# An encoder layer in float32: the chunked scans with one product for outputs and next state, and group norm by row sums

## The chip, the cores and the metric

One core of a Trainium2 chip runs the whole layer in one launch. The time is the device time of that core in microseconds. All matrix products are float32: a plain float32 product is issued as two instruction pairs (weight load and product), and the large ones are split by hand into a high and a low part.

## The reference, cut to what matters

```python
def rwkv7_branch(...):                       # T = 256 tokens, 16 heads of 64 channels
    ...
    o = wkv7_bidirectional(both(r_h), heads(decay), k_dir, both(v_h), both(kk), heads(a))
    mean = jnp.mean(o, axis=-1, keepdims=True)
    var = jnp.mean(jnp.square(o - mean), axis=-1, keepdims=True)
    o = ((o - mean) * lax.rsqrt(var + RWKV_GN_EPS)).reshape(B, T, RWKV_WIDTH)
    o = (o * gn_w.astype(jnp.float32) + gn_b.astype(jnp.float32)).astype(r.dtype)
    ...
    return (o + bonus) * g
```

`wkv7_bidirectional` is a linear recurrence over tokens with a 64x64 state per head, run forward and backward; the two results are added, the backward one turned round in time. What the layer does before it (a SwiGLU block, the input projection) and after it (the branch products with `w_branch_a` and `w_branch_b`, `w_out`, another SwiGLU block) is not touched.

## The kernel before, in words

Each engine has its own program; they meet at semaphores. Nearly all of the span is products of 128x128 weights with 512 moving columns (lines 1496 to 1498), whose matrices the SP queue loads into a ring of four slots; ScalarE makes the high part (`split_hi`, line 496) and VectorE the low part (`split_lo`, line 938). The next loads wait for the low part.

The scans are a stage of their own, 1328 to 1464 us. There are NM = 16 scans: m//2 is the pair of heads, m%2 the direction. A scan is cut into four chunks of 64 tokens. Data lie as channels by tokens (two heads on 128 partitions); for a backward scan the operands are stored or read in reversed order. For scan m:

- A (`alpha_beta`, lines 1785 and 1786) makes four 64x64 matrices per chunk and head; VectorE multiplies them by masks into `mb` (`masked_ab`, line 1352). Their decay ends come from `ends` (line 1251), which must be done before A of that scan (`dd_ready`).
- W (`w_products`, line 1811) multiplies them by the inverses `zs`; ScalarE copies the result with a minus sign into `wt` (`minus_w`, line 841).
- V (`values_t`, line 1801) turns the values by a product with the identity, chunk by chunk; ScalarE copies them beneath the state in `sv` (`values`, line 836).
- G (`gh_products`, lines 1826 and 1827) makes, per chunk and head, the matrix that takes state and values to outputs (64 columns) and to the next state (64 columns); VectorE masks it into `gh` (`masked_gh`, line 1361, two instructions of 128x512).
- R (`recur`) runs chunk after chunk: line 1842 multiplies `gh` by `sv` for the next state, which ScalarE copies into `sv` (line 869), and line 1846 multiplies `sv` by `gh` for the outputs, channels by tokens. VectorE brings outputs to `oc` (`to_oc`, lines 1370 and 1372), the backward ones reversed and added.

Group norm follows per pair of heads. `gn_means` and `gn_variances` (lines 1855, 1859) multiply `oc` and its squares by `headsum`, a matrix that adds the channels of a head and spreads the sum; VectorE subtracts (line 1318), ScalarE takes the square root over 128x256 (line 854), VectorE its reciprocal (line 1325), scales, adds and gates (lines 1326 to 1330). Then ScalarE and VectorE split the result into `yahi` and `yalo` (lines 859, 1334), weights of the branch product `p_ya`.

All is one order written out by hand. TensorE, for each m: W(m+1), V(m+1), then four times R(m,c) and A(m+2,c), with a group-norm product behind R(m,0), then G(m+1). VectorE, for each m: `ends(m+2)`, the two halves of `masked_ab(m+2)` with a part of the group norm between them (`norm_between`), `to_oc(m)`, the two halves of `masked_gh(m+1)`, and for m < 4 a weight split of `p_ya` (`ahead`). ScalarE, for each m: `minus_w(m+1)`, `values(m+1)`, three state copies, for m < 4 a weight split, and a part of the group norm. POOL loads values, bonus and gate per pair and copies `ik` and `vrev`.

Of the kernel before, what the change touches and what calls it, by code (L numbers as in the profile page):

```python
# [42 lines left out]
P = 128  # L43
# [45 lines left out]
def constants():  # L89
# [11 lines left out]
    k[:, K_MG:K_RESET] = np.concatenate([(p < C) | (s <= t), s >= -1 + 0 * t], 1)  # L101
# [10 lines left out]
def layer(nc, a, out):  # L112
# [94 lines left out]
    with ctx:  # L207
# [19 lines left out]
        def room(*names):  # L227
# [7 lines left out]
        s_g, (_, bo, gg, _, osq, rs) = room(("u_gap0", [P, NPAIR, T]), ("bo", [P, 4, T]), ("gg", [P, 4, T]),  # L235
                                            ("u_gap1", [P, NPAIR, T]), ("osq", [P, 2, T]), ("rs", [P, 2, T]))
# [4 lines left out]
        def ffn_room(tag):  # L241
# [93 lines left out]
        gn_mean, gn_cent, gn_sq, gn_var, gn_sqrt, ya_y, ya_hi, ya_lo = (  # L335
            sem(n) for n in ("gn_mean", "gn_cent", "gn_sq", "gn_var", "gn_sqrt", "ya_y", "ya_hi", "ya_lo"))
# [19 lines left out]
        lamb = sm[:, 57:63]  # L356

# [123 lines left out]
        def _(act):  # L481
# [350 lines left out]
            def values(m):  # L832
                act.wait_ge(vt_mm, m + 1)
                if m >= 2:
                    act.wait_ge(o_mm, m - 1)
                nc.scalar.activation(sv[C:P, m % 2, :, :], ps[C:P, 2, :].rearrange("p (c v) -> p c v", c=NC_),
                                     ACT.Copy).then_inc(vt_ready, 1)

            def minus_w(m):
                act.wait_ge(w_mm, m + 1)  # L840
                nc.scalar.activation(wt[:, m % 2, :, :], ps[:, 3, :].rearrange("p (c v) -> p c v", c=NC_),  # L841
                                     ACT.Copy, scale=-1.0).then_inc(w_ready, 1)

            def gn_square(b):
                act.wait_ge(gn_cent, b + 1)
                if b >= 2:
                    act.wait_ge(gn_var, b - 1)
                nc.scalar.activation(osq[:, b % 2, :], oc[:, b, :], ACT.Square).then_inc(gn_sq, 1)

            def gn_deviation(b):  # L850
                act.wait_ge(gn_var, b + 1)
                if b >= 2:
                    act.wait_ge(ya_y, b - 1)
                nc.scalar.activation(rs[:, b % 2, :], ps[:, 6, T:2 * T], ACT.Sqrt, scale=1.0 / C,
                                     bias=sm[:, GNE]).then_inc(gn_sqrt, 1)
# [7 lines left out]
            for m in range(NM):  # L863
# [3 lines left out]
                for c in range(NC_ - 1):  # L867
                    act.wait_ge(s_mm, 3 * m + c + 1)
                    nc.scalar.activation(sv[0:C, m % 2, c + 1, :], ps[0:C, 2, 0:2 * C], ACT.Copy).then_inc(s_ready, 1)
                if m < RING:  # L870
                    ahead(p_ya, [m])
                b = m // 2 - 1
                if m % 2:
                    if b >= 0:
                        gn_deviation(b)
                else:
                    if b >= 1:
                        ya_high(b - 1)
                    if b >= 0:
                        gn_square(b)  # L880
            gn_square(NPAIR - 1)
            ya_high(NPAIR - 2)
# [41 lines left out]
        def _(dve):  # L924
# [321 lines left out]
            def ends(m):  # L1246
# [4 lines left out]
                V.tensor_tensor(q[:, at:at + NC_, :], q[:, 0:1, :].broadcast_to((P, NC_, C)),  # L1251
# [61 lines left out]
            V.memset(sv[0:C, 0, 0, :], 0.0)  # L1313
            V.memset(sv[0:C, 1, 0, :], 0.0).then_inc(sv_zero, 1)

            def gn_center(b):
                dve.wait_ge(gn_mean, b + 1)
                V.scalar_tensor_tensor(out=oc[:, b, :], in0=ps[:, 6, 0:T], scalar=-1.0 / C, in1=oc[:, b, :],
                                       op0=ALU.mult, op1=ALU.add).then_inc(gn_cent, 1)

            def gn_scale(b):
                dve.wait_ge(gn_sqrt, b + 1)
                dve.wait_ge(gn_in[b % 4], 32 * (b // 4 + 1))
                y = oc[:, b, :]
# [11 lines left out]
            def norm_between(m):  # L1336

                b = m // 2 - 1
                if m % 2 == 0:
                    if b >= 1:  # L1340
                        gn_scale(b - 1)
                    if b >= 0:
                        gn_center(b)

            def masked_ab(m):
                for h in range(2):
# [3 lines left out]
                    if m >= 2 and h == 0:  # L1350
# [3 lines left out]
                                    kc[:, K_M1:K_MG].unsqueeze(1).broadcast_to((P, 2, 4 * C)), ALU.mult).then_inc(ab_ready, 1)  # L1354

            def masked_gh(m):
                for h in range(2):
                    dve.wait_ge(gh_mm, 2 * m + h + 1)
                    if m >= 2 and h == 0:
                        dve.wait_ge(o_mm, m - 1)  # L1360
                    V.tensor_tensor(gh[:, m % 2, 4 * h:4 * h + 4, :],
                                    ps[:, 4 + h, :].rearrange("p (c v) -> p c v", c=4),
                                    kc[:, K_MG:K_RESET].unsqueeze(1).broadcast_to((P, 4, 2 * C)), ALU.mult).then_inc(gh_ready, 1)

            def to_oc(m):
                b = m // 2
# [802 lines left out]
```

## Time and profile before

| | |
|---|---|
| times, us | 2388.73, 2391.84, 2391.40; median 2391.4 |
| profiled execution, us | 2389.68 |
| its span, us | 2387.9 |
| mean granted TensorE clock | 0.994 |
| busy, us | TensorE 2328.2, its weight loads 1904.5, VectorE 1503.0, ScalarE 1094.8, POOL 134.6 |

The span runs from the first to the last instruction of the profiled execution; the time of a run is some 2 us more. A group's mean is in ns, everything else in us. Starts are counted from the start of the span. Weight loads (PEld) and products (PE) overlap, so the distance between the starts of two groups on TensorE says more than their busy times.

### The profile page before, as it was taken

Reading aid. Unit: us, or ns where it says so; the run is one execution under the profiler, and the core shown is the slowest. Engines: PE = TensorE matmul, PEld = TensorE weight load, DVE = VectorE, ACT = ScalarE, POOL = GpSimd, SP = SyncE. Lnnn points to the kernel's source line nnn. Section 1 sums busy time; section 2 is a strip of 40 time slices with the busy share of each in tenths; the row PEclk is TensorE's granted clock in tenths of the full one; section 3 lists DMA queues with packets and bytes.
Section 4 is the critical chain, followed back from the end, with each engine's and each line's share of the span. In section 5 each row is a group of like instructions: output and inputs, shape, how many; then the busy total and the mean of one; then the engine's idle time right before and its main releaser. Section 6 shows DMA issues by size and latency. Waiting matters only on the chain.

```text
span 2387.9 us, 32654 instructions
## 1 busy us (share of the span) xinstructions
PE 2328.2 (98%) x12315; PEld 1904.5 (80%) x12315; DVE 1503.0 (63%) x1973; ACT 1094.8 (46%) x1431; POOL 134.6 (6%) x208
## 2 busy tenths in 40 slices
PE   8999999999998999999999999998999999999997
PEld 6888888888887877777777777887888888888886
DVE  5766754666656655987864456666667664476664
ACT  5454433444445654554556323444544443444442
POOL 1000000000001001321011210000000000000000
PEclk9999999999999999999999999999999999999999
DMA  7666666666665755678677212765666666666654
GB/s 245 200 191 196 188 199 194 191 194 190 197 190 194 210 159 165 206 214 282 188 223 208 92 45 99 232 235 154 211 193 190 196 193 194 195 190 196 193 187 141
DMA packets 229569, 451.18 MB, mean 189 GB/s; under 512 B 23372, under 2 KB 25696, under 8 KB 228048
## 3 DMA queue, kind: packets, MB, share of 16 engines
q1 hardware_dynamic: 207872, 399.82, 55.0%
q0 software_dynamic: 11472, 44.98, 5.7%
q10 hardware_dynamic: 10112, 4.83, 0.8%
q8 instruction: 76, 1.25, 0.2%
q14 instruction: 37, 0.30, 0.0%
HBM read 427.02 MB, written 22.54 MB: 188 GB/s over the span
## 4 chain that ended last, share of the span: by engine, by line
PE 63%; issue 30%; DVE 3%; ACT 2%; DMA 1%; POOL 0%; ACTq 0%; DVEq 0%; POOLq 0%
PE ps L1496 18%; PE ps L1497 18%; PE ps L1498 18%; PE ps L1785 1%; PE ps L1826 1%; PE ps L1811 1%; PE ps L1827 1%; DMA xin<-dif_dram 1%; PE ps L1786 1%; PE ps L1801 1%; PE ps L1842 1%; DVE wlo L938 0%; PE ps L1846 0%; PE ps L1521 0%; DMA n_dram<-nst 0%
## 5 line engine op out<-in xcount | busy, mean ns | idle before, releaser
L938 DVE TENSOR_TENSOR wlo<-raw,whi 128x1024 fp32r<-128x1024 f32 (+1 forms) x760 | 929.6, 1227 | 708.7 <-ACT whi L496 704.1
L496 ACT ACTIVATE whi<-raw 128x1024 fp32r<-128x1024 f32 (+1 forms) x760 | 801.5, 1058 | 962.4 <-PE ps L1498 929.7
L1496 PE MATMUL ps<-whi,uhi 128*128 128x512 f32 (+1 forms) x2272 | 898.1, 395 | 2.4 <-DVE ulo L977 2.0
L1497 PE MATMUL ps<-wlo,uhi 128*128 128x512 f32 (+1 forms) x2272 | 886.3, 390 | 0.0
L1498 PE MATMUL ps<-whi,ulo 128*128 128x512 f32 (+1 forms) x2272 | 885.2, 390 | 0.0
L1496 PEld LDWEIGHTS ps<-whi,uhi 128*128 128x128 f32 x2272 | 428.4, 189 | 101.5 <-issue 11.0
L1498 PEld LDWEIGHTS ps<-whi,ulo 128*128 128x128 f32 x2272 | 428.2, 188 | 89.6
L1497 PEld LDWEIGHTS ps<-wlo,uhi 128*128 128x128 f32 x2272 | 428.4, 189 | 84.3
L1496 PE MATMUL ps<-whi,hthi 128*128 128x512 f32 x704 | 273.9, 389 | 0.0
L1497 PE MATMUL ps<-wlo,hthi 128*128 128x512 f32 x704 | 273.9, 389 | 0.0
L1498 PE MATMUL ps<-whi,htlo 128*128 128x512 f32 x704 | 273.9, 389 | 0.0
L1034 DVE STREAM_TRANSPOSE hr<-hm 32x256 f32<-32x256 f32 x352 | 153.4, 436 | 5.7
L1496 PEld LDWEIGHTS ps<-whi,hthi 128*128 128x128 f32 x704 | 132.2, 188 | 27.6
L1497 PEld LDWEIGHTS ps<-wlo,hthi 128*128 128x128 f32 x704 | 132.2, 188 | 27.3
L1498 PEld LDWEIGHTS ps<-whi,htlo 128*128 128x128 f32 x704 | 132.2, 188 | 27.3
L1920 POOL TENSOR_TENSOR sm<-sm 128x2 f32<-128x2 f32 x6 | 8.8, 1470 | 1555.1 <-DVE sm L999 1483.8
L1352 DVE TENSOR_TENSOR mb<-ps,kc 128x512 f32<-128x512 f32 x32 | 22.1, 690 | 60.7 <-PE ps L1786 60.7
L523 ACT ACTIVATE uhi<-ps,vec 128x256 fp32r<-128x256 f32 x48 | 19.8, 473 | 31.0 <-PE ps L1521 31.0
L544 ACT ACTIVATE sg<-f 128x512 f32<-128x512 f32 x24 | 14.9, 623 | 39.5 <-DVE f L1049 29.1
L841 ACT ACTIVATE wt<-ps 128x512 f32<-128x512 f32 x16 | 9.6, 598 | 47.3 <-PE ps L1811 47.3
L1023 DVE SCALAR_TENSOR_TENSOR hm<-ps,sm,sg 128x512 f32<-128x512 f32 x44 | 30.9, 743 | 0.0
L1785 PE MATMUL ps<-q,beta 64*64 64x128 f32 x256 | 28.3, 292 | 2.5 <-issue 1.7
(268 smaller groups left out, 1461.7 us busy)
## 6 DMA issues: line engine op xcount, KB each, us to landing
raw<-in_ffn_w_gu SPq DMA_DIRECT2D x352, 512.0 KB, 4.5
raw<-in_ffn_w_down SPq DMA_DIRECT2D x176, 512.0 KB, 4.5
raw<-in_w_in SPq DMA_DIRECT2D x160, 512.0 KB, 3.9
raw<-in_w_out SPq DMA_DIRECT2D x32, 512.0 KB, 4.2
raw<-in_w_branch_a SPq DMA_DIRECT2D x16, 512.0 KB, 4.4
raw<-in_w_branch_b SPq DMA_DIRECT2D x16, 512.0 KB, 4.0
gate_dram<-gst_g POOLq DMA_DIRECT2D x8, 512.0 KB, 6.7
gbuf<-gate_dram POOLq DMA_DIRECT2D x8, 512.0 KB, 4.8
```

The source lines that it names most:

```text
L496: nc.scalar.activation(whi[:, s, :, 0:p.width], raw[:, s, :, 0:p.width], ACT.Copy).then_inc(hi_ready, 1)
L938: V.tensor_tensor(wlo[:, s, :, 0:p.width], raw[:, s, :, 0:p.width], whi[:, s, :, 0:p.width].bitcast(F32), ALU.subtract).then_inc(lo_ready, 1)
L1023: last = V.scalar_tensor_tensor(out=hm[:, t, :], in0=ps[:, 2 * gu.pair(1) + t, :], scalar=rstd(e, t), in1=sg[:, t, :], op0=ALU.mult, op1=A ...
L1034: last = V.transpose(dst[:, a], src[:, r])
L1496: mm(o, at, w_, start=(j == 0 and k == 0), stop=False)
L1497: mm(o, at, l_, start=False, stop=False)
L1498: last = mm(o, bt, w_, start=False, stop=(j == p.slots - 1 and k == SB - 1))
L1785: mm(o[:, 0:2 * C], beta[r, m, c * C:(c + 1) * C], q[r, at:dd + 1:dd - at, :], start=True, stop=True)
L1786: last = mm(o[:, 2 * C:4 * C], q[r, at + 2, :], q[r, 0:at + 2:at + 1, :], start=True, stop=True)
L1801: last = mm(ps[C:P, 2, c * P:(c + 1) * P], vt[:, c * C:(c + 1) * C], ident, start=True, stop=True)
L1811: last = mm(ps[r, 3, c * P:(c + 1) * P], zs[r, NC_ * m + c, :], mb[r, m % 2, c, 2 * C:4 * C], start=True, stop=True)
L1826: mm(o, wt[r, m % 2, c, :], mb[r, m % 2, c, 0:2 * C], start=True, stop=False)
```

## The change

- The masks and the halves of `ik`, `wt` and `sv` change places, so that in `gh` outputs are columns 0 to 63 and the next state columns 64 to 127, and values lie on partitions 0 to 63 of `sv`, the state on 64 to 127.
- R takes all 128 columns of `gh` as weights and 64 columns of `sv` as moving operand: one product per head and chunk, tokens by channels for the outputs, with the next state below them.
- For a backward scan the columns of tokens are read reversed (`scan_columns`), so outputs come in true order; `m1r` holds the reversed mask. `to_oc` is gone: ScalarE copies outputs (`outputs`), two instructions of 64x256 a scan, into `oc` or `ob`, tokens on the partitions.
- V is two transposes of 128x128, copied by two ScalarE instructions instead of one.
- Group norm adds the two directions and sums each head along the free dimension on VectorE (`gn_center`, `gn_variance`), root and reciprocal are over 128x4, `gn_scale` multiplies, two transposes (`gn_turn`) bring it back to channels by tokens, `ya_out` applies weight, bonus, bias and gate. The products with `headsum` in this stage go.
- On VectorE `gn_center` and `gn_scale` stand behind `masked_gh`; `gn_variance`, `ya_low` and `ya_out` between the halves of `masked_ab`. The last pair's norm moves from behind the start of `p_ya` to the end of the loop, and its transposes stand behind two steps of `p_ya`.

```diff
             def values(m):
...
-                nc.scalar.activation(sv[C:P, m % 2, :, :], ps[C:P, 2, :].rearrange("p (c v) -> p c v", c=NC_),
-                                     ACT.Copy).then_inc(vt_ready, 1)
+                for e in range(2):
+                    last = nc.scalar.activation(sv[0:C, m % 2, e::2, :],
+                                                ps[C * e:C * (e + 1), 2, 0:2 * P].rearrange("p (k v) -> p k v", v=P), ACT.Copy)
+                last.then_inc(vt_ready, 1)
...
+            def outputs(m):
+                b, d = m // 2, m % 2
+                act.wait_ge(o_mm, m + 1)
+                if d and b >= 2:
+                    act.wait_ge(gn_cent, b - 1)
+                chunks = ps[0:C, 7, :].rearrange("p (c v) -> p c v", c=NC_)
+                dst = (ob[:, b % 2, :] if d else oc[:, b, :]).rearrange("p (k v) -> p k v", v=P)
+                for e in range(2):
+                    last = nc.scalar.activation(dst[C * e:C * (e + 1), :, :],
+                                                chunks[:, ::-1, :][:, e::2, :] if d else chunks[:, e::2, :], ACT.Copy)
+                last.then_inc(o_ready, 1)
...
-                    nc.scalar.activation(sv[0:C, m % 2, c + 1, :], ps[0:C, 2, 0:2 * C], ACT.Copy).then_inc(s_ready, 1)
+                    nc.scalar.activation(sv[C:P, m % 2, c + 1, :], ps[C:P, 7, c * P:(c + 1) * P], ACT.Copy).then_inc(s_ready, 1)
+                    if c == 1 and m % 2 == 0 and m:
+                        gn_square(m // 2 - 1)
+                outputs(m)
...
             def gn_center(b):
-                dve.wait_ge(gn_mean, b + 1)
-                V.scalar_tensor_tensor(out=oc[:, b, :], in0=ps[:, 6, 0:T], scalar=-1.0 / C, in1=oc[:, b, :],
-                                       op0=ALU.mult, op1=ALU.add).then_inc(gn_cent, 1)
+                dve.wait_ge(o_ready, 2 * b + 2)
+                y = oc[:, b, :]
+                link(V.tensor_tensor(y, y, ob[:, b % 2, :], ALU.add))
+                link(V.tensor_reduce(GN_MEAN, by_head(y), AX.X, ALU.add))
+                link(V.tensor_scalar(GN_MEAN, GN_MEAN, 1.0 / C, None, ALU.mult))
+                V.tensor_tensor(by_head(y), by_head(y), GN_MEAN.unsqueeze(2).broadcast_to((P, 4, C)),
+                                ALU.subtract).then_inc(gn_cent, 1)
+
+            def gn_variance(b):
+                dve.wait_ge(gn_sq, b + 1)
+                V.tensor_reduce(GN_VAR, by_head(osq[:, b % 2, :]), AX.X, ALU.add).then_inc(gn_ms, 1)
 
             def gn_scale(b):
                 dve.wait_ge(gn_sqrt, b + 1)
+                y = by_head(oc[:, b, :])
+                link(V.reciprocal(GN_DEV, GN_DEV))
+                V.tensor_tensor(y, y, GN_DEV.unsqueeze(2).broadcast_to((P, 4, C)), ALU.mult).then_inc(gn_scaled, 1)
+
+            def ya_out(b):
+                dve.wait_ge(gn_t, b + 1)
...
             def norm_between(m):
-                b = m // 2 - 1
                 if m % 2 == 0:
-                    if b >= 1:
-                        gn_scale(b - 1)
-                    if b >= 0:
-                        gn_center(b)
+                    if m:
+                        gn_variance(m // 2 - 1)
+                    if m >= 4:
+                        ya_low(m // 2 - 2)
+                elif m >= 3:
+                    ya_out((m - 3) // 2)
+
+            def norm_behind(m):
+                if m % 2:
+                    gn_center(m // 2)
+                elif m:
+                    gn_scale(m // 2 - 1)
...
-                if m % 2 and m >= 5:
-                    ya_low(m // 2 - 2)
-                to_oc(m)
-                dve.wait_ge(o_ready, m + 1)
                 if m + 1 < NM:
                     masked_gh(m + 1)
+                norm_behind(m)
                 if m < RING:
                     ahead(p_ya, [m])
...
                 vt = vrev if d else vb
-                for c in range(NC_):
-                    last = mm(ps[C:P, 2, c * P:(c + 1) * P], vt[:, c * C:(c + 1) * C], ident, start=True, stop=True)
+                for k in range(NT):
+                    last = nc.tensor.transpose(ps[:, 2, k * P:(k + 1) * P], vt[:, k * P:(k + 1) * P], ident)
                 last.then_inc(vt_mm, 1)
...
-                if c < NC_ - 1:
-                    for h in range(2):
-                        last = mm(ps[0:C, 2, h * C:(h + 1) * C], gh[:, m % 2, NC_ * h + c, C:2 * C],
-                                  sv[:, m % 2, c, h * C:(h + 1) * C], start=True, stop=True)
-                    last.then_inc(s_mm, 1)
                 for h in range(2):
-                    last = mm(ps[C * h:C * (h + 1), 7, c * C:(c + 1) * C], sv[:, m % 2, c, h * C:(h + 1) * C],
-                              gh[:, m % 2, NC_ * h + c, 0:C], start=True, stop=True)
-                if c == NC_ - 1:
-                    last.then_inc(o_mm, 1)
...
+                    last = mm(ps[:, 7, c * P + h * C:c * P + (h + 1) * C], gh[:, m % 2, NC_ * h + c, :],
+                              sv[:, m % 2, c, h * C:(h + 1) * C], start=True, stop=True)
+                last.then_inc(s_mm if c < NC_ - 1 else o_mm, 1)
+
+            def gn_turn(b):
+                pe.wait_ge(gn_scaled, b + 1)
...
+                for k in range(NT):
+                    last = nc.tensor.transpose(ps[:, 6, k * P:(k + 1) * P], oc[:, b, k * P:(k + 1) * P], ident)
+                last.then_inc(gn_t, 1)
...
                 for c in range(NC_):
                     recur(m, c)
-                    if c == 0 and m >= 2:
-                        gn_means(m // 2 - 1) if m % 2 == 0 else gn_variances(m // 2 - 1)
+                    if c == 0 and m >= 3 and m % 2:
+                        gn_turn((m - 3) // 2)
                     if m + 2 < NM:
                         alpha_beta(m + 2, c)
...
-            gn_means(NPAIR - 1)
             fill = filler(in_steps(p_ya, product(p_ya, lambda u, k: yahi[:, k, :], lambda u, k: yalo[:, k, :],
                                                  lambda j: pe.wait_ge(ya_lo, SB * (j + 1))), [], []))
-            fill(1)
-            gn_variances(NPAIR - 1)
-            fill(15)
+            fill(2)
+            gn_turn(NPAIR - 1)
+            fill(14)
```

## Rows read from the trace of the kernel before

**Rows 1.** The page, busy time: us, share of the span, instructions of each engine.

```profile
PE 2328.2 (98%) x12315; PEld 1904.5 (80%) x12315; DVE 1503.0 (63%) x1973; ACT 1094.8 (46%) x1431; POOL 134.6 (6%) x208
```

**Rows 2.** Stretches: bounds, length, each engine's busy us (instructions), clock, DMA share, GB/s.

```profile
1398.46:1407.88 9.42, 8.55 (x120) 6.89 (x119) 6.35 (x11) 2.75 (x7) 1.55 (x4) 1.00 0.01 2
1407.88:1416.36 8.48, 8.48 (x119) 6.90 (x119) 3.94 (x8) 2.36 (x6) 1.67 (x4) 1.00 0.48 172
```

**Rows 3.** Timeline of TensorE, W products of units 0, 2, 5, 14: start, us, engine, line.

```profile
1328.24 1.09 PE L1811 MATMUL ps<-mb,zs 64*64 64x128 f32 x16
...
1345.01 1.09 PE L1811 MATMUL ps<-mb,zs 64*64 64x128 f32 x16
...
1372.08 1.09 PE L1811 MATMUL ps<-mb,zs 64*64 64x128 f32 x16 [0.87 <-DVE mb L1352]
...
1452.16 1.09 PE L1811 MATMUL ps<-mb,zs 64*64 64x128 f32 x16
```

**Rows 4.** The timeline of TensorE at the end of unit 7 and in unit 8.

```profile
1395.52 0.34 PE L1846 MATMUL ps<-gh,sv 128*64 128x64 f32 x4
1395.78 0.44 PE L1785 MATMUL ps<-q,beta 64*64 64x128 f32 x4
...
1396.37 0.50 PE L1826 MATMUL ps<-mb,wt 64*128 64x128 f32 x4
...
1399.48 0.76 PE L1801 MATMUL ps<-kc,vrev 128*64 128x128 f32 x5
1399.97 0.27 PE L1842 MATMUL ps<-sv,gh 128*64 128x64 f32 x1
...
1400.61 0.70 PE L1855 MATMUL ps<-oc,kc 128*128 128x256 f32 x2
1401.24 0.44 PE L1785 MATMUL ps<-q,beta 64*64 64x128 f32 x4
...
1401.83 0.39 PE L1842 MATMUL ps<-sv,gh 128*64 128x64 f32 x3
...
1402.32 0.44 PE L1785 MATMUL ps<-q,beta 64*64 64x128 f32 x4
```

**Rows 5.** The timeline of VectorE in unit 8.

```profile
1398.52 1.29 DVE L1361 TENSOR_TENSOR gh<-ps,kc 128x512 f32<-128x512 f32 x2 [0.66 <-DVE oc L1370]
1399.72 0.41 DVE L1251 TENSOR_TENSOR q<-q,pend 128x256 f32<-128x256 f32 x1
...
1403.65 1.74 DVE L1325 RECIPROCAL rs<-rs 128x256 f32<-128x256 f32 x1
```

**Rows 6.** Groups by line and form: count, busy us, mean ns, idle before; last, min/median/max.

```profile
L1846 PEld LDWEIGHTS ps<-gh,sv 128*64 128x64 f32 x256 | 16.2, 136 | 3.2 <-issue 2.4 <-ACT sv L869 0.8
...
L869 ACT ACTIVATE sv<-ps 64x128 f32<-64x128 f32 x48 | 13.0, 271 | 29.8 <-PE ps L1842 29.4
...
L836 ACT ACTIVATE sv<-ps 64x512 f32<-64x512 f32 x15 | 8.9, 592 | 6.1 <-PE ps L1801 6.1
...
L1855 PEld LDWEIGHTS ps<-oc,kc 128*128 128x128 f32 x14 | 2.1, 188 | 0.5
...
L1267 DVE RECIPROCAL su<-su 128x4 f32<-128x4 f32 x8 | 1.4, 171 | 0.0
...
L1521 PE MATMUL ps<-kc,mg x32: 270/272/273, 1536.4 to 1564.5; 128*128 128x128 f32 x32
```

**Rows 7.** The chain of waits in unit 1: start, us, what.

```profile
1337.79 1.13 DVE wlo L938
```

**Rows 8.** Timeline of TensorE in units 14 and 15; last, the waits behind: us, times, longest.

```profile
1455.24 0.39 PE L1842 MATMUL ps<-sv,gh 128*64 128x64 f32 x3 [0.23 <-ACT sv L869]
...
1456.05 0.39 PE L1842 MATMUL ps<-sv,gh 128*64 128x64 f32 x3 [0.24 <-ACT sv L869]
...
1464.19 0.70 PE L1855 MATMUL ps<-oc,kc 128*128 128x256 f32 x2 [0.52 <-DVE oc L1370]
...
PEld ps L1496 <- DVE ulo L1334: 0.5, 1, 0.5
```

More of the change, by code:

```diff
@@ L356, in layer, with scan_columns, by_head @@
         lamb = sm[:, 57:63]
+        GN_MEAN, GN_VAR, GN_DEV = sm[:, 0:4], sm[:, 4:8], sm[:, 8:12]
+        def scan_columns(m):
+            return slice(None, None, -1) if m % 2 else slice(None)
+        def by_head(a):
+            return a.rearrange("p (g v) -> p g v", v=C)
         def slot_of(p, u, j):
@@ L846, in gn_square @@
                 if b >= 2:
-                    act.wait_ge(gn_var, b - 1)
+                    act.wait_ge(gn_ms, b - 1)
                 nc.scalar.activation(osq[:, b % 2, :], oc[:, b, :], ACT.Square).then_inc(gn_sq, 1)
             def gn_deviation(b):
[L851 to L855, printed above, removed]
+                act.wait_ge(gn_ms, b + 1)
+                nc.scalar.activation(GN_DEV, GN_VAR, ACT.Sqrt, scale=1.0 / C, bias=sm[:, GNE]).then_inc(gn_sqrt, 1)
             def ya_high(b):
@@ L1330, in gn_scale @@
-                V.tensor_tensor(y, y, gg[:, b % 4, :], ALU.mult).then_inc(ya_y, 1)
+                link(V.scalar_tensor_tensor(out=y, in0=ps[:, 6, 0:T], scalar=vec[:, R_GNW + b:R_GNW + b + 1],
+                                            in1=bo[:, b % 4, :], op0=ALU.mult, op1=ALU.add))
+                V.scalar_tensor_tensor(out=y, in0=y, scalar=vec[:, R_GNB + b:R_GNB + b + 1], in1=gg[:, b % 4, :],
+                                       op0=ALU.add, op1=ALU.mult).then_inc(ya_y, 1)
             def ya_low(b):
@@ L1353, in masked_ab @@
                                     ps[:, h, :].rearrange("p (c v) -> p c v", c=2),
-                                    kc[:, K_M1:K_MG].unsqueeze(1).broadcast_to((P, 2, 4 * C)), ALU.mult).then_inc(ab_ready, 1)
+                                    (m1r[:, :] if m % 2 else kc[:, K_M1:K_MG]).unsqueeze(1).broadcast_to((P, 2, 4 * C)),
+                                    ALU.mult).then_inc(ab_ready, 1)
             def masked_gh(m):
@@ L1360, in masked_gh @@
                         dve.wait_ge(o_mm, m - 1)
[L1361 to L1366, printed above, removed]
-                dve.wait_ge(o_mm, m + 1)
-                src = ps[:, 7, 0:T]
-                if m % 2:
-                    V.tensor_tensor(oc[:, b, :], oc[:, b, :], src[:, ::-1], ALU.add).then_inc(o_ready, 1)
-                else:
-                    V.tensor_copy(oc[:, b, :], src).then_inc(o_ready, 1)
+                    mask = by_head(kc[:, K_MG:K_RESET])[:, :, scan_columns(m)]
+                    V.tensor_tensor(gh[:, m % 2, 4 * h:4 * h + 4, :].rearrange("p c (w t) -> p c w t", w=2),
+                                    ps[:, 4 + h, :].rearrange("p (c w t) -> p c w t", c=4, w=2),
+                                    mask.unsqueeze(1).broadcast_to((P, 4, 2, C)), ALU.mult).then_inc(gh_ready, 1)
             for m in range(2):
@@ L1384, in _ @@
                     norm_between(m)
-                if m % 2 and m >= 5:
-                    ya_low(m // 2 - 2)
-                to_oc(m)
-                dve.wait_ge(o_ready, m + 1)
                 if m + 1 < NM:
                     masked_gh(m + 1)
+                norm_behind(m)
                 if m < RING:
                     ahead(p_ya, [m])
-            gn_center(NPAIR - 1)
-            gn_scale(NPAIR - 2)
             ya_low(NPAIR - 2)
+            gn_variance(NPAIR - 1)
+            gn_scale(NPAIR - 1)
+            ya_out(NPAIR - 1)
+            ya_low(NPAIR - 1)
             def merge_a(c):
@@ L1429, in _ @@
             fill(RING)
-            gn_scale(NPAIR - 1)
-            ya_low(NPAIR - 1)
             fill(4)
@@ L1826, in gh_products @@
                         mm(o, wt[r, m % 2, c, :], mb[r, m % 2, c, 0:2 * C], start=True, stop=False)
-                        last = mm(o, ik[r, c, :], q[r, at:dd + 1:dd - at, :], start=False, stop=True)
+                        last = mm(o, ik[r, c, :], q[r, at:dd + 1:dd - at, scan_columns(m)], start=False, stop=True)
                         if c == NC_ - 1:
```

59 lines of the change are left out of this document (23 added, 36 removed).

## The prediction

> **What bounds the kernel now.** I read first the page's busy shares: TensorE is busy 98% of the span [rows 1]. Only the scan stage is touched, 1328 to 1464 us, so I took the table of stretches there, then the timeline of one unit. I call unit m the turn of scan m on TensorE, from the first W product (L1811) to the next unit's: W, V (values, L1801), then four steps of R (recurrence, L1842 and L1846) and A (L1785, L1786), then G (L1826, L1827). An even unit takes 9.42 us, with TensorE busy 8.55, an odd one 8.48 and busy throughout [rows 2]. The reader is to see two things. TensorE is paced by its own stream: an R-and-A step repeats every 1.08 us (A at 1401.24 and 1402.32), the last, from R to G, takes 0.85 (1395.52 to 1396.37, unit 7), and 0.63 goes to the group-norm product (1400.61 to 1401.24) [rows 4]. The even unit's missing 0.9 us is W waiting for the second mask, which stands on VectorE behind a reciprocal of 1.74 us [rows 5]. The order of VectorE's queue counts as much: `ends` (L1251) starts right behind the two masks of G, at 1399.72, and releases the next A [rows 5].
>
> **The change part by part.** Times are from a unit's first W product.
>
> *Values.* Eight instructions of about 0.12 us ((0.76-0.27)/4) become two transposes, one instruction each, 0.27 long alone [rows 4, 6]. But R must wait for both masks of G. They start 0.06 into the unit, take 1.29, and R starts at 1.51 [rows 4, 5]. W ends at 1.02, so V ends near 1.25 and TensorE waits: values gain nothing in the loop. Only ahead of the loop, where V(0) stands alone, do six instructions go: -0.6 us.
>
> *One product for outputs and state.* Per step there were 8 instructions with 64-column weights, now 4 with 128-column weights over 64 moving columns. A 64-column load shows 0.136 us, a 128-column one 0.188 [rows 6]; the 0.052 between them for 64 more columns makes a 128-column load 0.107 of stream. Today R takes 0.49 (1401.83 to 1402.32) and the last R, without state, 0.26 (1395.52 to 1395.78) [rows 4]. In each change of array shape the next group starts some 0.07 before the last product's end (the 128-wide pair of 1400.61 is shown 0.70 long and A starts at 0.63) [rows 4]. New R: a first load of 0.107, three more of 0.107, the last product of 0.22 (0.39 for three at 0.055 spacing leaves about that) minus 0.07: 0.58. Bounds: 0.49, as the narrow group now, and 0.74, if each product's 0.053 of streaming adds to its load. I take 0.58, as the 128-wide loads of 1400.61 cost no more. A stays 0.59. So a step is 1.17 instead of 1.08, and the last one 1.17 instead of 0.85: from R of step 1 to the next W, with G at 2.09 (1396.37 to 1398.46, where unit 8 starts), 3x1.17+2.09=5.60 instead of 2x1.08+0.85+2.09=5.10. That is **+0.5 a unit**.
>
> The Trainium skill (TensorE: Matmul & The Clock Gate, LDWEIGHTS) counts a load by its columns, P/1.2 ns: 107 ns for 128, and the 0.052 step agrees. The Trainium skill's page TensorEngine Tiling (Array Packing), When to Use Tiling, advises for 64 moving columns to swap the operands and tile the columns: that is how L1846 stands before the change, and what the change gives up. By that rule alone R would be best left at its 0.49 and 0.26; the bounds above have that too.
>
> *Group norm on TensorE.* The 0.63 after R(m,0) goes from every unit from 2 on; every odd unit gets two transposes, about 0.2. What is late next? First ScalarE: W's last product is shown until 1.09 [rows 3], its copy (128x512, 0.6) runs to 1.74, and values are now two copies. From 0.592 for 64x512 and 0.271 for 64x128 [rows 6], a 64x256 one is 0.38, so values end at 2.46 instead of 2.3, the state copy at 2.73, and R of step 1 can't start before 2.8. Second, and worse, **VectorE's queue**: `norm_behind` stands between the G masks and the next `ends`.
> - Behind an odd scan, that is at the start of an even unit: `gn_center`: add 0.42 and reduce 0.42 (L1251's size shows 0.41 [rows 5]; a reduce of this size isn't shown), scale 0.17 (as four elements in rows 6), subtract 0.33 to the next issue (L1251 starts 0.09 before the masks end), three hand-overs of about 0.03: 1.44. It starts at 1.26; `ends` takes 0.44 more: 3.14, A at 3.20, R1 at 3.79. Bounds 1.2 to 1.9 for the centring (all at the 0.33 spacing, or each full width plus a slower reduce).
> - Behind an even scan: `gn_scale`, 0.17+0.04+0.34=0.55; the transposes wait for it until 1.96, A at 2.3, R1 at 2.90.
>
> Today R1 starts at 3.37 (1401.83) [rows 4]. Units from 5 on: even 3.79+5.60=9.39 against 9.42 (its 0.9 us wait goes: in the gap between the masks now stand 0.8 us, the 1.74 reciprocal has become 0.17), odd 8.50 against 8.48 to 8.55. Nine units: about **-0.3 us**.
>
> *Units 0 to 4.* Here VectorE also does a weight split of 1.13 us behind the masks [rows 7]; today it hides the group norm's product. Unit 0: 2.8+5.6=8.4. Unit 1: 1.26+1.13+0.44+0.06=2.89, R1 3.47: 9.07, as the split set it before too. Together 17.47 against 1345.01-1328.24=16.77 [rows 3]: **+0.7**. Units 2 and 4: centring and split add: 1.26+1.44+1.13+0.44+0.06=4.33, R1 4.92, 10.52 each. Unit 3: 9.63. Together 30.67 against 1372.08-1345.01=27.07 [rows 3]: **+3.6**. That is the largest term.
>
> *End.* In units 14 and 15 no A stands between steps, and state copy and R alternate: 0.81 now (1455.24 to 1456.05) [rows 8], then 0.65+0.04+0.27+0.06=1.02. From unit 14's start: R1 at 2.84 (now 3.08), two steps of 1.02, G at 5.46, ends 7.55, masks, R(15,0) at 9.05, three steps to 12.11, first product of the branch about 12.6. Now the product of 1464.19 stands there, 0.43 of stream from 12.03: 12.5 to 12.6. Even. Behind it the second moments' product (0.43) becomes the transposes (0.2), and the wait of 0.5 for the last remainder [rows 8] goes: from R's end the new chain (two output copies 0.76, centring 1.6, square 0.46, sum 0.45, root 0.25, scale 0.65) is 4.2 us, under two steps of the branch (5.5), and the rest (2.0) under the third. **-0.7**.
>
> POOL's copies and the vb loads keep their places and have over 2 us to spare. The reversed masks, `m1r` (made while VectorE idles 10 us ahead of the stage) and the 4-d view of G's masks I cost at 0; bound for the view 0 to 0.1 an instruction, since the masks gate R in every unit. Reversed moving operands cost 0 (bounds -0.05 to +0.05 a unit).
>
> **Sum.** -0.6+0.7+3.6-0.3+0.0-0.7=+2.7 us. Against the profiled execution (2389.7 us, span 2387.9) 2392.4; the median of the runs shown is 1.7 higher, so 2394.1.
>
> **Rivals.**
> 1. *Wide loads are not hidden* (slower): R 0.74, +0.16 in some 62 steps, +10: 2404. For it: R's products are short, 0.053 against loads of 0.107, so little can hide. Against: in the pair of 1400.61 two loads and a first stream of 256 columns, all in a row, would put the second product's end at 0.107+0.213+0.107+0.378=0.80; shown is 0.70, so its load was hidden [rows 4]. The Trainium skill (TensorE: Matmul & The Clock Gate, Part 3: Packing small matmuls) has it as a rule that a load overlaps running products only where the row groups differ; that pair speaks against the rule. The mechanism decides from 0.62 a step on (+0.034x62 makes 2.1 more, 4.8 in all).
> 2. *The centring is hidden* (faster): if VectorE's queue did not hold A, even units 2 to 12 would start R1 at 2.9 instead of 3.8 to 4.9, -0.9 to -2.0, together -8, and with R at 0.52 some -4 more: 2383. For it: only that small VectorE durations may overlap more than I count. Against: `ends` stands behind it in program order.
> 3. *R is as cheap as the narrow group*, 0.49: -0.09x62=-5.6: 2388.5, no measurable change.
> 4. *The masks get dearer* (0.1 each for strips of 64): +0.2 over 16 units, with two longer output copies on ScalarE: 2398, slower.
> 5. *Recurrence wins by fewer instructions*: the change does what it says, but what it removes (0.63 a unit) only uncovers the queue wait; that is my forecast itself.
>
> **How the numbers follow.** A change under 0.2% (4.8 us) can't be told from none. Forecast, 2394.1, 0.46 (0.34 of it within 0.2%, 0.12 over, its own range 2390 to 2398); rival 1 0.17; rival 2 0.15; rival 3 0.12; rival 4 0.10. Faster 0.15, same 0.34+0.12=0.46, slower 0.12+0.17+0.10=0.39. The range drops the far halves of rivals 1 and 2: 2385 to 2402.
>
> **What would show it.** R to A at 0.58 with the step at 1.17 (0.49 and 0.74 are the rivals); A of even units released by `ends`, near 3.2, and near 4.3 in units 2 and 4; R(m,0) still at 1.5; no wait of W for the mask; no wait for the last remainder. It is wrong if even units are under 9.0 us or units 2 and 4 under 10.

## The result and the profile after

| | before | after |
|---|---|---|
| median of the runs, us | 2391.1 | 2415.6 (2413.1 to 2417.0, four runs) |
| profiled execution, its span | 2389.7, 2387.9 | 2413.1, 2411.3 |
| mean granted TensorE clock | 0.994 | 0.983, in each of the four runs |

The ratio is 1.0103, its 95% interval 1.0090 to 1.0115: 24.5 us slower, where 2.7 were forecast and 2402 was the end of the range. The median before is of four runs, the three shown ahead of the prediction (2391.4) and one more.

The page's second part has it in one line: the clock in tenths, which stood at 9 everywhere before, falls in the slices of the scan stage.

```profile
PEclk9999999999999999999999988999999999999999
```

The table of stretches, one for each unit (2, 4, 5, 6, 8, 9, 10 and 12 shown; columns as in [rows 2], the granted clock third from the right), says where:

```profile
1344.53:1355.13 10.60, 8.21 (x99) 6.80 (x98) 5.89 (x11) 4.98 (x11) 0.74 (x2) 1.00 0.16 49
...
1364.71:1379.58 14.87, 12.53 (x99) 10.30 (x99) 6.23 (x12) 3.52 (x10) 0.74 (x2) 0.66 0.11 36
1379.58:1388.05 8.47, 8.47 (x101) 6.97 (x100) 4.40 (x9) 3.23 (x9) 1.95 (x4) 1.00 0.19 49
1388.05:1401.68 13.63, 12.37 (x100) 10.23 (x99) 5.16 (x12) 3.52 (x10) 0.74 (x2) 0.66 0.00 1
...
1410.47:1419.90 9.43, 8.22 (x100) 6.78 (x99) 5.09 (x12) 3.52 (x10) 0.74 (x2) 1.00 0.01 2
1419.90:1428.37 8.47, 8.47 (x102) 6.98 (x101) 4.40 (x10) 3.22 (x9) 2.46 (x5) 1.00 0.50 173
1428.37:1440.87 12.50, 11.29 (x100) 9.43 (x99) 5.10 (x12) 3.52 (x10) 0.74 (x2) 0.73 0.01 2
...
1449.33:1462.83 13.50, 12.29 (x100) 10.17 (x99) 5.17 (x12) 3.52 (x10) 0.74 (x2) 0.67 0.00 0
```

Units 4, 6, 10 and 12 are longer than their like (unit 2 for unit 4, unit 8 for the others). Unit 6 does what unit 8 does, with as many instructions, in 13.63 us instead of 9.43, at a clock of 0.66 instead of 1.00. Units that ran at 1.00 came out as forecast:

| unit | 0 | 1 | 2 | 3 | 5 | 8 | 9 |
|---|---|---|---|---|---|---|---|
| forecast, us | 8.40 | 9.07 | 10.52 | 9.63 | 8.50 | 9.39 | 8.50 |
| measured, us | 8.36 | 9.03 | 10.60 | 9.58 | 8.47 | 9.43 | 8.47 |

The timeline of TensorE in units 8 and 4 answers to [rows 4]:

```profile
1410.47 1.09 PE L1845 MATMUL ps<-mb,zs 64*64 64x128 f32 x16
1411.50 0.44 PE L1835 MATMUL ps<-kc,vrev 128*128 128x128 f32 x2
1411.82 0.66 PE L1875 MATMUL ps<-sv,gh 128*128 128x64 f32 x4
1413.68 0.44 PE L1819 MATMUL ps<-q,beta 64*64 64x128 f32 x4 [1.21 <-DVE q L1270]
1413.95 0.39 PE L1820 MATMUL ps<-q 64*64 64x128 f32 x4
1414.28 0.66 PE L1875 MATMUL ps<-sv,gh 128*128 128x64 f32 x4
```

```profile
1366.05 0.66 PE L1875 MATMUL ps<-sv,gh 128*128 128x64 f32 x4
1369.05 0.70 PE L1819 MATMUL ps<-q,beta 64*64 64x128 f32 x4 [2.34 <-DVE q L1270]
1369.54 0.64 PE L1820 MATMUL ps<-q 64*64 64x128 f32 x4
1370.11 1.11 PE L1875 MATMUL ps<-sv,gh 128*128 128x64 f32 x4
1371.15 0.70 PE L1819 MATMUL ps<-q,beta 64*64 64x128 f32 x4
```

The reader is to see in unit 8 the wait for `ends` in brackets, A at 3.21 (1413.68-1410.47; forecast 3.20), and R as a group of four instructions, shown 0.66 long. In unit 4, after a wait of 2.34 us, the same groups are longer: A and R repeat every 2.10 us (1369.05 to 1371.15) where they take 1.18 at full clock. That is the lower of the clock's two levels, 1.2 GHz, as the stretch that begins inside the wait shows:

```profile
1368.50:1378.70 10.20, 9.65 (x64) 7.97 (x66) 2.54 (x6) 2.01 (x6) 0.00 (x0) 0.50 0.17 53
```

VectorE's timeline in unit 8, which answers to [rows 5], shows what `ends` (L1270) stood behind: add, sum, scale and subtract of the centring.

```profile
1410.47 1.29 DVE L1407 TENSOR_TENSOR gh<-ps,kc 128x512 f32<-128x512 f32 x2 [1.27 <-PE ps L1861]
1411.68 0.41 DVE L1339 TENSOR_TENSOR oc<-oc,ob 128x256 f32<-128x256 f32 x1
1412.13 0.42 DVE L1340 TENSOR_REDUCE sm<-oc 128x4 f32<-128x256 f32 x1
1412.58 0.25 DVE L1341 TENSOR_SCALAR sm<-sm 128x4 f32<-128x4 f32 x1
1412.87 0.43 DVE L1342 TENSOR_TENSOR oc<-oc,sm 128x256 f32<-128x256 f32 x1
1413.21 0.42 DVE L1270 TENSOR_TENSOR q<-q,pend 128x256 f32<-128x256 f32 x1
```

### The profile page after: what moved, and what is told of

It is laid out like the page before. It is cut to its first block, busy times and chain, and to the rows that moved or that the text cites. A ratio compares the mean times of both kernels' runs of the same rounds, so it can differ in the third digit from the quotient of the medians.

```text
span 2411.3 us, 32111 instructions
## 1 busy us (share of the span) xinstructions
PE 2345.9 (97%) x12011; PEld 1921.5 (80%) x12011; DVE 1497.0 (62%) x1991; ACT 1107.5 (46%) x1479; POOL 134.9 (6%) x208
## 3 DMA queue, kind: packets, MB, share of 16 engines
q8 instruction: 74, 1.21, 0.2%
## 4 chain that ended last, share of the span: by engine, by line
PE 62%; issue 30%; DVE 4%; ACT 2%; DMA 1%; POOL 0%; ACTq 0%; DVEq 0%; POOLq 0%
PE ps L1530 18%; PE ps L1532 18%; PE ps L1531 18%; PE ps L1875 2%; PE ps L1819 1%; DVE wlo L957 1%; PE ps L1860 1%; PE ps L1861 1%; PE ps L1820 1%; DMA xin<-dif_dram 1%; PE ps L1555 0%; DMA n_dram<-nst 0%; PE ps L1845 0%; DVE h L1027 0%; PE ps L1684 0%
## 5 line engine op out<-in xcount | busy, mean ns | idle before, releaser
L1875 PE MATMUL ps<-sv,gh 128*128 128x64 f32 x256 | 46.6, 309 | 3.7 <-ACT sv L891 2.2
L1875 PEld LDWEIGHTS ps<-sv,gh 128*128 128x128 f32 x256 | 37.4, 210 | 15.2 <-ACT sv L891 8.3
L1407 DVE TENSOR_TENSOR gh<-ps,kc 128x512 f32<-128x512 f32 x32 | 20.6, 686 | 28.5 <-PE ps L1861 28.5
L1396 DVE TENSOR_TENSOR mb<-ps,kc 128x512 f32<-128x512 f32 x16 | 11.1, 692 | 42.1 <-PE ps L1820 42.0
L1860 PE MATMUL ps<-mb,wt 64*128 64x128 f32 x256 | 35.7, 332 | 0.0
```

The costliest lines, as they stand in the source:

```text
L1407: V.tensor_tensor(gh[:, m % 2, 4 * h:4 * h + 4, :].rearrange("p c (w t) -> p c w t", w=2), ps[:, 4 + h, :].rearrange("p (c w t) -> p c w t ...
L1860: mm(o, wt[r, m % 2, c, :], mb[r, m % 2, c, 0:2 * C], start=True, stop=False)
L1875: last = mm(ps[:, 7, c * P + h * C:c * P + (h + 1) * C], gh[:, m % 2, NC_ * h + c, :], sv[:, m % 2, c, h * C:(h + 1) * C], start=True, sto ...
```

## The experiments

Two theories for the low clock. **W**: TensorE's waits for `ends`, 1.2 us in even units and 2.4 in units 2 and 4, make it. **P**: the wide product with its short streams makes it, waits or not. Each kernel was timed beside the kernel before, whose median was 2390.3 to 2391.1 us in all of these; the ratios are against it.

**e1_order.** The centring behind the next `ends`.

```diff
                 if m + 2 < NM:
                     ends(m + 2)
+                if m and m % 2 == 0:
+                    norm_behind(m - 1)
+                if m + 2 < NM:
                     masked_ab(m + 2)
...
-                norm_behind(m)
+                if m % 2 == 0:
+                    norm_behind(m)
...
+            norm_behind(NM - 1)
```

> The changed kernel with one edit on VectorE: in even units the centring stands behind the next ends instead of ahead of it. Theory W (the waits of TensorE for ends, 1.2 us in even units and 2.4 us in units 2 and 4, let the granted clock fall to its lower level): with the waits gone the clock stays at 1.00 through the stage, R of step 1 comes at 2.9 in even units, each takes 8.5 us, units 2 and 4 about 9.1, and the time is 2387 to 2389. Theory P (the wide recurrence product and its short streams load TensorE too little, whatever the waits): the clock still falls for tens of microseconds and the time is 2400 or more.

**e2_narrow.** R as two products side by side in the column halves.

```diff
                 for h in range(2):
-                    last = mm(ps[:, 7, c * P + h * C:c * P + (h + 1) * C], gh[:, m % 2, NC_ * h + c, :],
-                              sv[:, m % 2, c, h * C:(h + 1) * C], start=True, stop=True)
+                    for w in range(2):
+                        last = mm(ps[C * w:C * (w + 1), 7, c * P + h * C:c * P + (h + 1) * C],
+                                  gh[:, m % 2, NC_ * h + c, C * w:C * (w + 1)],
+                                  sv[:, m % 2, c, h * C:(h + 1) * C], start=True, stop=True)
```

> The changed kernel with R as two products per head and chunk again, 64 columns of weights each, side by side in the two column halves of the array; the same values and the same order. At full clock I expect R at about 0.37 to 0.42 us instead of 0.59, a step at 0.98, so some 12 us less if nothing else changed. Theory W: the waits for ends stay, so the clock still falls in the stage and the time is 2398 to 2406. Theory P: the clock stays at 1.00 and the time is about 2382.

**e3_fill.** The waits kept and filled.

```diff
+                    if c == 0:
+                        for _ in range({1: 1, 2: 5, 3: 2, 4: 5}.get(m, 2 if m % 2 == 0 and 6 <= m < 14 else 0)):
+                            mm(ps[:, 6, T:2 * T], ident, kc[:, 0:T], start=True, stop=True)
```

> The changed kernel, its waits kept but filled: behind R(m,0) TensorE does products of 0.43 us each whose result nobody reads, five in units 2 and 4, two in unit 3 and in even units 6 to 12, one in unit 1, all of them within the wait for ends. Theory W (idle time of TensorE lowers the clock): the clock stays at 1.00, the units keep the lengths of my prediction (9.4 even, 8.5 odd, 10.6 in units 2 and 4) and the time is 2392 to 2397, the forecast. Theory P: little changes, 2410 to 2416.

**e4_before_wait.** The waits alone, in the kernel before (`pad` is a spare tile that nobody reads).

```diff
                     masked_gh(m + 1)
+                if m % 2 and m < 13:
+                    for _ in range(5):
+                        link(V.tensor_tensor(pad[:, :], kc[:, 0:T], kc[:, 0:T], ALU.add))
```

> The kernel before with five chained VectorE additions of 128x256 on a spare tile (2.25 us) behind the masks of G of every odd scan, which hold the next ends and so A of even units: the waits of the changed kernel in the old kernel, with its narrow products. Waits alone cost about 1.2 us in units 6 to 12 and 2.3 in units 2 and 4: 9.4 us, 2400.5. Theory W: the clock falls here too, time 2408 to 2422. Theory P: the clock stays at 1.00, time 2400.

Measured: e1 2393.4 us (1.0019, 1.0008 to 1.0030), e2 2392.2 (1.0006, 0.9996 to 1.0016), e3 2398.6 (1.0038, 1.0024 to 1.0052), e4 2403.9 (1.0055, 1.0038 to 1.0071). One stretch of 120 us in the middle of the stage, for the kernel before, the change, e1, e2, e3 and e4 in this order, one fence each:

```profile
1330.00:1450.00 120.00, 114.23 (x1596) 92.43 (x1590) 67.09 (x113) 38.88 (x91) 19.41 (x42) 1.00 0.16 50
```

```profile
1330.00:1450.00 120.00, 109.68 (x1168) 90.84 (x1170) 56.72 (x112) 43.23 (x112) 15.92 (x35) 0.89 0.15 47
```

```profile
1330.00:1450.00 120.00, 115.38 (x1325) 94.78 (x1325) 65.19 (x130) 50.31 (x132) 21.44 (x42) 0.97 0.16 50
```

```profile
1330.00:1450.00 120.00, 106.83 (x1577) 84.52 (x1574) 65.24 (x130) 50.12 (x131) 18.88 (x42) 0.97 0.16 50
```

```profile
1330.00:1450.00 120.00, 117.86 (x1330) 96.15 (x1330) 62.96 (x126) 48.49 (x128) 18.80 (x42) 1.00 0.15 48
```

```profile
1330.00:1450.00 120.00, 107.43 (x1441) 87.28 (x1436) 72.37 (x131) 34.97 (x81) 18.68 (x37) 0.96 0.15 48
```

A mean of 0.89 over 120 us is 26 us at half clock (120x0.11x2); 0.97 is 7, 0.96 is 10. What follows: filling the waits, with order and product as they were, restores the clock there (e3), so it is idle time of TensorE that costs it. P, which holds waits or not, is out.

W as I put it is too simple. e1 should have come to 2387 to 2389 by W and 2400 or more by P; 2393.4 is neither. It keeps waits of 1.0 us behind the weight splits in units 2, 3 and 4, and one low stretch of some 7 us begins 1.5 us behind that of unit 2; the other two passed. e2 kept all the waits and had 7 us at half clock here, in units 2 and 4, not 26; I had expected 2398 or more and got 2392.2. e4 has the waits in the old kernel and shows one low stretch, of some 10 us, at the wait of 2.46 us in unit 4. Its waits of 1.3 us passed at full clock, and so did one of 2.51 us in unit 2:

```profile
1351.62 0.44 PE L1788 MATMUL ps<-q,beta 64*64 64x128 f32 x4 [2.51 <-issue]
```

I had expected 2408 or more of e4 and got 2403.9. e3 came out above its range of 2392 to 2397, and not at 1.00 throughout: a fall was left in units 14 and 15, where state copy and R alternate.

**e5_before_wide.** The wide product alone, in the kernel before. This kernel leaves out what turns the outputs back to channels by tokens, so it does not compute the layer; it is there for its time.

```diff
-                    nc.scalar.activation(sv[0:C, m % 2, c + 1, :], ps[0:C, 2, 0:2 * C], ACT.Copy).then_inc(s_ready, 1)
+                    nc.scalar.activation(sv[0:C, m % 2, c + 1, :], ps[C:P, 7, c * P:(c + 1) * P], ACT.Copy).then_inc(s_ready, 1)
...
-                if c < NC_ - 1:
-                    for h in range(2):
-                        last = mm(ps[0:C, 2, h * C:(h + 1) * C], gh[:, m % 2, NC_ * h + c, C:2 * C], ...
-                    last.then_inc(s_mm, 1)
                 for h in range(2):
-                    last = mm(ps[C * h:C * (h + 1), 7, c * C:(c + 1) * C], sv[:, m % 2, c, h * C:(h + 1) * C], ...
-                if c == NC_ - 1:
-                    last.then_inc(o_mm, 1)
+                    last = mm(ps[:, 7, c * P + h * C:c * P + (h + 1) * C], gh[:, m % 2, NC_ * h + c, :],
+                              sv[:, m % 2, c, h * C:(h + 1) * C], start=True, stop=True)
+                last.then_inc(s_mm if c < NC_ - 1 else o_mm, 1)
```

> The kernel before with the wide product alone: R multiplies all 128 columns of gh by sv, and the next state is copied from partitions 64 to 127 of its result. Outputs then come tokens by channels and nothing turns them back, so the outputs of the scans are not in the reference's layout; group norm and the rest work on them as they are. Full clock: R 0.59, +0.5 us a unit, and R(m,0) can no longer start beside the tail of V, up to +0.4 more: 10 to 13 us, 2400 to 2404. If a wide product alone is enough to lower the clock (P), there are low stretches in the middle of the stage and the time is 2410 or more; if waits are needed too (W), the clock is 1.00 between 1330 and 1450 us.

**e6_order2.** e1, and the four splits of `p_ya` behind `ends` as well.

```diff
+                if 0 < m <= RING:
+                    ahead(p_ya, [m - 1])
...
-                if m < RING:
-                    ahead(p_ya, [m])
```

> The first experiment's order, and the four weight splits on VectorE also behind ends. Full clock: units 1 to 4 take 8.5 to 8.6 us instead of 9.1, about -2.2 us in all, and the low stretch at 1351 us of the first experiment goes with the 1 us waits of units 1 to 4 if waits make it: 2387 to 2390. If the wide product makes it, it stays and the time is 2391.

**e10_order2_narrow** is e6 with the product of e2; **e7_best** is that with `values(m + 1)` moved behind the first state copy on ScalarE:

```diff
                     minus_w(m + 1)
-                    values(m + 1)
                 for c in range(NC_ - 1):
...
+                    if c == 0 and m + 1 < NM:
+                        values(m + 1)
```

> The kernel with ends first and R as two products side by side, but ScalarE's copy of the next values ahead of the first state copy, as in the change. The state copy then ends at 2.7 us instead of 2.2, R of step 1 at 2.8 instead of 2.5 us into the unit: units of 7.85 instead of 7.5, +4 to +5 us on the kernel with the late copy (2374.9): 2378 to 2380. If the copies of values are hidden in either place, the two are equal.

> Ends ahead of centring and of the weight splits, R as two products side by side, and ScalarE's copy of the next values behind the first state copy instead of ahead of it. R 0.39 and R of step 1 at 2.5: units of 7.5 us against 8.95 before, some -17 us over units 1 to 13 at full clock: 2374. TensorE has short waits in units 14 and 15 only, where the low stretch of some 10 us stays (+4): 2376 to 2380. If short streams alone lower the clock, low stretches appear between 1330 and 1430 us too: 2382 or more.

**e8_best_fill** adds to e7 products that nobody reads ahead of the stage and in its last two units; **e9_fill_all** adds such products to the changed kernel in all its waits. `feed(n, wide, bank)` issues n of them, of 0.43 us each where wide and 0.21 where not; the diff is that of e8.

```diff
+            feed(2, 1, 7)
             w_products(0)
+            feed(2, 1, 7)
             values_t(0)
...
                     recur(m, c)
+                    if m >= NM - 2 and c < NC_ - 1:
+                        feed(1, 0)
...
                     gh_products(m + 1)
+                if m == NM - 2:
+                    feed(2, 1)
```

> The same kernel with products nobody reads in the waits of TensorE ahead of the stage (two ahead of W(0), two ahead of V(0)) and in units 14 and 15 (0.21 us behind each of six R, two of 0.43 ahead of R(15,0)). They cost at most 1 us where they overrun a wait. Theory W: no low stretch is left between 1320 and 1480 us and the time is 3 to 5 us under that of the kernel without them. Otherwise the two are equal or this one is up to 1 us slower.

> The changed kernel with its own order and its wide product, and unread products in all waits of TensorE: those of the third experiment, and in addition two ahead of W(0), two ahead of V(0), one of 0.43 us behind each of the first three R of units 14 and 15, two ahead of R(15,0). If the low clock is all that my forecast missed, the clock is 1.00 from 1320 to 1500 us and the time is that of the forecast, 2391 to 2395, 4 to 7 us under the third experiment. If low stretches stay though TensorE is kept busy, the waits are not what makes them, and the time stays near 2398.

| kernel | order on VectorE | product | median, us | ratio to before (95%) |
|---|---|---|---|---|
| the change | centring, split, ends | wide | 2415.6 | 1.0103 (1.0090 to 1.0115) |
| e9, all waits filled | the same | wide | 2394.9 | 1.0017 (1.0008 to 1.0027) |
| e5, old kernel, outputs not turned back | old | wide | 2400.4 | 1.0047 (1.0030 to 1.0064) |
| e6 | ends, centring, split | wide | 2386.4 | 0.9989 (0.9979 to 0.9999) |
| e10 | ends, centring, split | narrow | 2377.8 | 0.9953 (0.9937 to 0.9970) |
| e7, values late | ends, centring, split | narrow | 2374.9 | 0.9939 (0.9920 to 0.9958) |
| e8, e7 filled | ends, centring, split | narrow | 2369.3 | 0.9913 (0.9897 to 0.9930) |

The stretch from 1330 us in e5 and in e9, and the last part of the stage in the change, in e3 and in e9:

```profile
1330.00:1450.00 120.00, 118.01 (x1341) 96.58 (x1341) 63.07 (x105) 36.37 (x84) 18.00 (x39) 1.00 0.15 48
```

```profile
1330.00:1450.00 120.00, 117.86 (x1335) 96.16 (x1333) 62.97 (x125) 48.27 (x126) 17.40 (x39) 1.00 0.15 48
```

```profile
1450.00:1490.00 40.00, 35.31 (x284) 29.29 (x281) 17.53 (x42) 12.96 (x37) 3.98 (x8) 0.76 0.10 34
```

```profile
1450.00:1490.00 40.00, 36.64 (x236) 30.30 (x236) 19.56 (x38) 15.80 (x34) 2.41 (x4) 0.83 0.21 67
```

```profile
1450.00:1490.00 40.00, 39.54 (x303) 32.30 (x303) 23.09 (x43) 17.46 (x36) 3.94 (x7) 1.00 0.26 84
```

e5: the wide product leaves the clock at 1.00 in this stretch and costs 10.1 us on its own, as expected (10 to 13). Only at the end of the stage, from 1474 to 1478 us, does e5 show a short low stretch, behind waits of 1.33, 0.36 and 0.51 us.

e9: with every wait filled the clock is 1.00 in the whole stage, and the changed kernel, slower products, late `ends` and all, takes 2394.9 us; the forecast was 2394.1. So 20.7 of the 21.5 us that I missed are the clock. The units bear it out. From W of unit 0 to W of unit 14, in the change and in e9:

```profile
1327.14:1471.76 144.62, 132.87 (x1385) 109.89 (x1384) 67.17 (x133) 51.49 (x135) 18.82 (x42) 0.87 0.14 41
```

```profile
1331.61:1459.83 128.22, 126.08 (x1427) 102.88 (x1427) 67.13 (x133) 51.49 (x135) 18.80 (x42) 1.00 0.15 47
```

The forecast for these fourteen units was 128.2.

e6 was to take 2387 to 2390 and took 2386.4. e6 and e10 against each other put the wide product at 8.6 us. e7 is 3.0 us under e10 where I expected 4 to 5; with four runs each, 2374.2 to 2380.4 and 2370.4 to 2377.5, that difference is not clear of the noise. The timeline of e7 shows R 0.38 us before the next group (1391.53 to 1391.91) and units of 7.85 and 7.37:

```profile
1382.29 1.09 PE L1851 MATMUL ps<-mb,zs 64*64 64x128 f32 x16
...
1390.14 1.09 PE L1851 MATMUL ps<-mb,zs 64*64 64x128 f32 x16
...
1391.53 0.45 PE L1882 MATMUL ps<-sv,gh 128*64 128x64 f32 x8
1391.91 0.44 PE L1825 MATMUL ps<-q,beta 64*64 64x128 f32 x4
...
1397.51 1.09 PE L1851 MATMUL ps<-mb,zs 64*64 64x128 f32 x16
```

The median of e8 is 5.6 us under that of e7, by work that nobody needs; 3 to 5 were expected. It is less firm than e9: the runs of e8 lie from 2367.9 to 2371.3, one of the four of e7 is at 2370.4, and the two profiled executions are only 1.4 us apart (2371.3 and 2372.7). In these the clock of the last units is 1.00 in e8 and 0.94 in e7:

```profile
1430.00:1460.00 30.00, 28.73 (x282) 22.69 (x281) 16.86 (x33) 13.94 (x31) 1.83 (x3) 1.00 0.20 65
```

```profile
1430.00:1460.00 30.00, 26.52 (x259) 21.13 (x259) 16.04 (x33) 12.39 (x31) 1.83 (x3) 0.94 0.16 51
```

e8 is the fastest of all, 21 us under the kernel before; e7 is 15 us under it without a wasted product.

## Why the prediction was wrong

- *Which way:* the sum said +2.7 us and that this could not be told from no change. It is +24.5, clearly slower.
- *The step that failed* is one that was not there: every term of the sum priced its units at full clock, the +3.6 of units 2 to 4, the -0.3 of units 5 to 13 and the end alike, and the clock was put at nothing without a reason. I worked out waits of 1.2 and 2.4 us for TensorE and took them at their length. They cost their length, and some of them a stretch of several us at half clock as well: unit 4 took 14.87 instead of 10.52, unit 6 13.63 instead of 9.39, unit 10 12.50, unit 12 13.50. Against e9, units 0 to 13 lose 16.4 us (144.6 to 128.2), units 14 and 15 lose 1.5 (13.97 to 12.45, up to the first product of the branch), and the first thirteen products of the branch lose 2.6 (5.67 to 3.08), as they still run at the low level (below). Together that is 20.5; e9, which takes only idle time away, gives 20.7 us back: shown.

TensorE's timeline of the changed kernel at the end of the stage shows the products of the branch 0.43 us apart until 1491, and 0.22 to 0.24 apart from 1491.40 on:

```profile
1484.86 1.11 PE L1875 MATMUL ps<-sv,gh 128*128 128x64 f32 x4 [0.36 <-ACT sv L891]
...
1490.14 0.63 PE L1531 MATMUL ps<-wlo,uhi 128*128 128x512 f32 x1
1490.57 0.63 PE L1532 MATMUL ps<-whi,ulo 128*128 128x512 f32 x1
1491.00 0.56 PE L1530 MATMUL ps<-whi,uhi 128*128 128x512 f32 x1
1491.40 0.39 PE L1531 MATMUL ps<-wlo,uhi 128*128 128x512 f32 x1
1491.62 0.39 PE L1532 MATMUL ps<-whi,ulo 128*128 128x512 f32 x1
1491.86 0.40 PE L1530 MATMUL ps<-whi,uhi 128*128 128x512 f32 x1
```

- *VectorE's queue* ("second, and worse"): right, and the largest term was +3.6; measured at full clock units 2 and 3 are 10.60 and 9.58. The four-element scale took 0.25 instead of 0.17 and the centring 1.53 instead of 1.44, but it began at 1.21 instead of 1.26, so A came at 3.21 for 3.20.
- *R(m,0)* came at 1.35, not at the 1.51 that I had put among the signs. The masks of G end at 1.35 in the kernel before too (1399.81); what held R until 1.51 there was V, still running in [rows 4]. So the transposes did bring R(m,0) forward by 0.16, and it earned nothing: in an even unit A waits for `ends`, in an odd one the transposes of group norm wait for the scale.
- *The wide product:* 0.58 forecast, 0.59 measured, the step 1.18 for 1.17. The 0.74 of rival 1 did not come, so it is out.
- *The wait of W for the mask* went as said. `outputs` did not set the pace: in unit 8 ScalarE is idle for 0.91 us before it, and behind it and the root for 2.62 us.
- *Two terms were mis-sized, by less than 1 us each.* V ahead of the loop was to give -0.6 and gave about -0.1 (W(0) to W(1) takes 6.49 before, 6.37 after): the shorter V only waits longer for its values, which I had said had over 2 us to spare. The nine units from 5 on took 80.08 before (1452.16-1372.08) and 5x8.50+4x9.39 is 80.06, so my own numbers gave 0.0 there and not -0.3. At full clock (e9) the change costs 4.0 us against the kernel before, not 2.7. Also, twice the 0.052 of a load's step is 0.104 and not 0.107, which over the four loads of a step of R is 0.01 us. V(0) before and after:

```profile
1323.19 1.09 PE L1801 MATMUL ps<-kc,vb 128*64 128x128 f32 x8 [0.35 <-DMA vb<-v_dram]
```

```profile
1322.75 0.44 PE L1835 MATMUL ps<-kc,vb 128*128 128x128 f32 x2 [0.89 <-DMA vb<-v_dram]
```

- *Rival 2* (the centring hidden, 2383) did not happen by itself, but it is near what e6 makes by moving the centring and the splits behind `ends`: 2386.4.
- *The range* was built from sizes of steps and had no room for the clock. No rival had the clock in it, though the profile before shows its granted clock in each row of the table of stretches, and the change makes gaps in TensorE's work: 114.2 us busy of the 120 before, 109.7 after, though part of these 109.7 is products stretched by the low clock.

From 1368.5 to 1378.7 us the trace grants 0.50, behind a wait of 2.34. The Trainium skill (TensorE: Matmul & The Clock Gate, A second HAM failure mode: psum-queue depth-cycling) tells of a bf16 kernel with products of 512 columns whose TensorE goes idle for moments between groups of products, and whose clock swings between its two levels for it. By that rule the trace agrees, and it belonged among my rivals.

Open: how waits and work add up, and why one wait lowers the clock and its like does not. The waits of the changed kernel with narrow products (e2) or in the old kernel (e4) cost 7 and 10 us of low clock in the middle stretch, the wide product without waits none, both together 26. That the narrow products leave fewer or shorter low stretches fits with shorter units around each wait, but no run separates it. The low stretches are read from one execution of each kernel; of the change, all four runs have the same mean clock, 0.983. Group norm by row sums and values by transposes were not timed alone.

## What to carry to other kernels

When a change opens a wait on the engine that sets the time, price it twice: its length, and the clock that it may cost; look up the granted clock of the stretch before and leave room for it. A helper's work queued ahead of a hand-over (`norm_behind` ahead of `ends`) cost most of this change's loss: moving that one call gave 22.2 of 24.5 us back by the medians (e1; three of its ten runs are 4 to 7 us above its median), and with the splits moved too and the products narrow the loss is a gain of 13 us (e10). Fewer instructions are not less time: R as four instructions with 128-column weights took 0.59 us, as eight with 64-column weights in two column halves 0.38.

## What the runs showed of the hardware that I had not expected

- Products whose result nobody reads made a kernel faster: 20.7 us in e9 against the change, and 5.6 us in e8 against e7 (less firm, as said).
- The length of one wait does not decide alone. A wait of 1.21 us was passed at full clock in unit 8, while unit 6, with one of 1.26, fell to half. A wait of 2.51 us was passed in unit 2 of e4, while one of 1.05 us in unit 2 of e1 was followed by a low stretch. The waits in unit 6 of the change and in unit 2 of e1:

```profile
1391.31 0.44 PE L1819 MATMUL ps<-q,beta 64*64 64x128 f32 x4 [1.26 <-issue]
```

```profile
1349.35 0.44 PE L1824 MATMUL ps<-q,beta 64*64 64x128 f32 x4 [1.05 <-issue]
```

- Eight products of 64-column weights in two column halves take 0.38 us from start to the next group, four of 128-column weights 0.59, the old mixed order 0.49, all at full clock.
- A VectorE scale of 128x4 elements behind a reduce took 0.25 us or a little more in six of its eight calls (L1341) and 0.17 in the last two, which stand behind a reduce as well; reciprocals of that size took 0.17 [rows 6]. What makes the difference is open.
